# Latent attention: VectorE instead of ScalarE copies the last transposed probabilities of each head

## The reference, cut to what matters

```
for each block of 128 queries i (kv_len = (i+1)*128):
    s = q_nope @ k_nope^T + q_rope @ k_rope^T, times (64+32)^-0.5
    p = softmax(where(causal mask, s, -inf))
    o = p @ v                                   # 16 heads, v of width 64
o = o * silu(gate);  return o @ w_out
```

## Time and profile before

| | us |
|---|---|
| median of 3 runs | 1749.3 |
| lowest and highest | 1748.59, 1751.31 |
| the profiled execution, its own time | 1748.29 |
| its span, first to last instruction | 1746.5 |
| TensorE busy in the span | 1695.5 |
| VectorE busy | 1016.4 |
| ScalarE busy | 842.5 |
| GpSimd busy | 701.0 |

### The profile page before, as it was taken

One profiled execution on the slowest core, in us unless ns is written; L12 is line 12 of the kernel. 1 busy time (PEld: TensorE's weight loads), 2 busy tenths in 40 slices (PEclk: granted clock), 3 DMA queues, 4 the chain that ended last, 5 costly groups with the idle time before them and its releaser, 6 DMA issues.

```text
span 1746.5 us, 24655 instructions
## 1 busy us (share of the span) xinstructions
PE 1695.5 (97%) x8729; PEld 1380.8 (79%) x8729; DVE 1016.4 (58%) x1600; ACT 842.5 (48%) x1472; POOL 701.0 (40%) x795
## 2 busy tenths in 40 slices
PE   8999999989999999999989999999999999999998
PEld 6877777757786667878878888888888888888887
DVE  5578685687458855376658657877634443222222
ACT  5465665786366654356532345565423331313131
POOL 2634445426442014411123432324345455555554
PEclk9999999999999999999999999999999999999999
DMA  7362624223231002201048521112133223333333
GB/s 223 109 193 77 189 85 121 86 84 85 77 90 45 17 20 81 61 25 37 25 154 256 180 61 37 49 49 61 49 97 97 84 85 97 97 96 96 96 97 109
DMA packets 217151, 160.55 MB, mean 92 GB/s; under 512 B 8334, under 2 KB 190615, under 8 KB 217047
## 3 DMA queue, kind: packets, MB, share of 16 engines
q1 hardware_dynamic: 201758, 125.50, 25.0%
q10 hardware_dynamic: 15288, 33.66, 5.8%
HBM read 156.98 MB, written 2.16 MB: 91 GB/s over the span
## 4 chain that ended last, share of the span: by engine, by line
PE 65%; issue 12%; DVE 8%; ACT 7%; POOL 7%; DMA 1%; ACTq 0%; POOLq 0%; DVEq 0%; SPq 0%
PE ps L665 14%; PE ps L669 14%; PE ps L666 14%; POOL wl L615 7%; PE ps L3184 3%; PE ps L3182 3%; PE ps L3181 3%; PE ps L2238 2%; PE ps L2220 1%; PE ps L1685 1%; ACT wh L628 1%; PE ps L1653 1%; PE ps L2777 1%; PE ps L2227 1%; PE ps L2743 1%
## 5 line engine op out<-in xcount | busy, mean ns | idle before, releaser
L615 POOL TENSOR_TENSOR wl<-raw,wh 128x256 fp32r<-128x256 f32 (+1 forms) x775 | 677.6, 905 | 985.8 <-ACT wh L628 985.8
L665 PE MATMUL ps<-ah,wh 128*128 128x512 f32 (+1 forms) x1144 | 457.2, 400 | 8.3 <-DVE al L793 2.2
L669 PE MATMUL ps<-ah,wl 128*128 128x512 f32 (+1 forms) x1144 | 446.7, 390 | 0.2
L666 PE MATMUL ps<-al,wh 128*128 128x512 f32 (+1 forms) x1144 | 445.7, 390 | 0.0
L628 ACT ACTIVATE wh<-raw 128x1024 fp32r<-128x1024 f32 (+1 forms) x220 | 230.6, 1049 | 299.2 <-PE ps L669 153.3
L665 PEld LDWEIGHTS ps<-ah,wh 128*128 128x128 f32 (+1 forms) x1144 | 213.6, 187 | 62.5 <-issue 8.6
L669 PEld LDWEIGHTS ps<-ah,wl 128*128 128x128 f32 (+1 forms) x1144 | 213.4, 187 | 49.2 <-POOL wl L615 1.9
L666 PEld LDWEIGHTS ps<-al,wh 128*128 128x128 f32 (+1 forms) x1144 | 213.7, 187 | 43.8 <-issue 1.7
L665 PE MATMUL ps<-bh,wh 128*128 128x512 f32 (+1 forms) x332 | 134.1, 404 | 8.1 <-DVE merged L2639 2.8
L669 PE MATMUL ps<-bh,wl 128*128 128x512 f32 (+1 forms) x332 | 130.8, 394 | 0.8 <-POOL wl L615 0.7
L666 PE MATMUL ps<-bl,wh 128*128 128x512 f32 (+1 forms) x332 | 130.0, 392 | 0.0
(11 more groups left out here) (470 smaller groups left out, 2965.4 us busy)
## 6 DMA issues: line engine op xcount, KB each, us to landing
raw<-w_mlp SPq DMA_DIRECT2D x64, 512.0 KB, 3.9
raw<-w_in SPq DMA_DIRECT2D x52, 512.0 KB, 3.8
raw<-ssm_w_in SPq DMA_DIRECT2D x40, 512.0 KB, 3.9
ada_late<-w_ada ACTq DMA_DIRECT2D x16, 1024.0 KB, 7.0
ada_raw<-w_ada ACTq DMA_DIRECT2D x16, 512.0 KB, 4.7
cum_rows<-cum_saved ACTq DMA_DIRECT2D x16, 512.0 KB, 3.9
raw<-ssm_w_out SPq DMA_DIRECT2D x16, 512.0 KB, 3.4
raw<-mla_w_in SPq DMA_DIRECT2D x11, 512.0 KB, 4.0
```

What stands on the lines that cost most here:

```text
L615: nc.gpsimd.tensor_tensor(wl[:, s, part], raw[:, s, part], wh[:, s, part].bitcast(F32), ALU.subtract).then_inc(lo_ready, LOW_PIECES * (par ...
L665: nc.tensor.matmul(dst, w_hi[k], x_hi[k], start=k == 0, stop=False)
L666: nc.tensor.matmul(dst, w_hi[k], x_lo[k], start=False, stop=False)
L669: ins = nc.tensor.matmul(dst, w_lo[k], x_hi[k], start=False, stop=k == n - 1)
```

## The change

The copy of part 2 of each head goes from ScalarE's queue to VectorE's. VectorE makes it for head h-2 in `softmax(h)`, behind the second division, as one `tensor_copy` of 128x512 out of bank 6; in the last step it makes the two that are left. It waits for the transpose and, from head 2 on, for the outputs that read the same buffer. Part 0 and 1 stay on ScalarE.

```diff
                     exp(h + 1, 0)
                     exp(h + 1, 1)
-                if h:
-                    copy_turned(h - 1, 2)
                 if h + 1 < MH:
                     exp(h + 1, 2)
                     exp(h + 1, 3)
...
                 copy_turned(h, 1)
-            copy_turned(MH - 1, 2)
             gate_high(MH // 2 - 1)
...
+            def copy_last(h):
+
+                dve.wait_ge(sem("probs_turned"), h * 3 + 3)
+                if h > 1:
+                    dve.wait_ge(sem("o_ready"), h // 2)
+                nc.vector.tensor_copy(probs_t[h % 2][:, 0:TT, 3 * P:T], bank(6).rearrange("p (k n) -> p k n", n=P)).then_inc(sem("probs_copied"), 1)
+
             def softmax(h):
                 for t in range(TT):
                     top(h, t)
                     if t >= 2:
                         scale(h, t - 2)
+                if h > 1:
+                    copy_last(h - 2)
                 scale(h, TT - 2)
                 scale(h, TT - 1)
...
             for h in range(MH):
                 if h + 1 < MH:
                     softmax(h + 1)
+                else:
+                    copy_last(h - 1)
+                    copy_last(h)
                 if h % 2 == 0 and h:
                     gate(h // 2 - 1)
```

## The result

The changed kernel takes 1756.50 us (median of 6 runs, 1755.65 to 1759.36) against 1748.96 us for the kernel before in the same series: a ratio of 1.0043, 95% interval 1.0031 to 1.0055. It is slower by 7.5 us. Forecast were 1756.7 us, from a median before of 1749.3, and 7.4 us slower. The profiled execution took 1755.93 us with a span of 1754.1, 7.6 us over the span of before.

The account below looks back on a forecast made before the run. TensorE, busy 97% of the span, was taken as the bound. Delays of 2.08 + 5.04 + 0.19 + 0.09 gave 7.4 us slower, 1756.7 us against a median of 1749.3; range 1751 to 1763.

Parts of the forecast that it names:

- The copy starts 0.27 us behind the second division and takes 0.69: VectorE's queue: free 0.27 us after the second division's start; copy priced at 0.69 us from another 128x512 PSUM copy.
- Work starts 1.02 us behind the second division: TensorE's outputs or first transposes start 1.02 us after VectorE's second division starts, 0.06 us behind the copy's end.
- the replay: Attention loop retimed step by step from the timelines before, with the copy on VectorE: 7.4 us slower; chance 0.72.
- The queue is pushed by 0.41 us: VectorE's queue behind the copy: second to fourth division takes 1.60 us instead of 1.19, so 0.41 later, not 0.62.
- Steps 5 to 8: +0.71, +1.65, +2.19, +2.52: TensorE's running delay over four attention steps; 2.52 us per four steps, repeated by the next four.
- In step 7 ScalarE's queue shifts by 1.23 us: Fourth exponential, after head 8's fourth maximum, starts 1.23 us later; queries, weight split, gate and head 7's first copy follow.
- First four heads 2.08, last heads 0.19 and 0.09: Delays outside the eight replayed steps: +2.08 us first four, +0.19 at last heads' transposes, +0.09 for the final copy.
- Twelve stalls of 0.5 to 1.1 us, 9 to 12 in all: Profile sign: TensorE waits for VectorE's probs_t before outputs and first transposes, replacing 4.3 us of waits for ScalarE.
- ScalarE 9.6 us less busy, VectorE 11 more: Profile sign: moving the copies makes ScalarE 9.6 us less busy and VectorE 11 us more.
- the one in which VectorE's lateness accumulates: Second division of every step: no old wait absorbs VectorE's lateness; 11.4 us slower, 1760.7 us; chance 0.13.
- The rival of no measurable difference: Later waits inside the stage take the stalls back, or the copy starts at once; 0 to +3 us, 1751; chance 0.09.
- The one on the other side: Copy ready before TensorE's projection ends, so only ScalarE's relief remains; 4.7 us faster, 1744.6 us; chance 0.06.

Follow-up runs that it names:

- The run with the load alone: Kernel before plus an unrelated VectorE multiplication, as long as the copy, at its place in fourteen of sixteen heads; copies stay on ScalarE: 1751.30 us, ratio 1.0010.
- the run of the even heads: Changed kernel with only even heads' copies on VectorE, behind the second division; odd heads' copies back on ScalarE: 1749.32 us, ratio 0.9998 to the kernel before.
- that of the odd heads: Changed kernel with only odd heads' copies on VectorE, behind the second division; even heads' copies back on ScalarE: 1757.21 us, ratio 1.0040 to the kernel before.
- the run ahead of the first division: Changed kernel with VectorE's copy ahead of the first division instead of behind the second: 1752.82 us, ratio 1.0018 to the kernel before.
- the run with ScalarE's copy late: Kernel before with ScalarE's copy moved behind the fourth exponential, nothing given to VectorE: 1759.21 us, ratio 1.0055.

## Why the prediction was right

- **Nothing is given back outside the loop.** Forecast 7.4 us; the loop gave 7.5, the span 7.6, the medians 7.5. That the sum is off by only 0.1 us is partly luck: the terms below are too small by 0.2 us before step 12 and too large by 0.1 behind it, and the medians can't show 0.1 us at all.
- **The copy starts 0.27 us behind the second division and takes 0.69.** Measured 0.27 and 0.684 on average. VectorE's copy of another tile and line priced this one within 1%.
- **Work starts 1.02 us behind the second division.** Right for the outputs (582.02 to 583.03 is 1.01). For the transposes it is 1.10 (575.55 to 576.65): they followed 0.15 us behind the copy, not 0.06. This costs nothing, as the scores then followed 0.68 us behind the transposes (576.65 to 577.33) and not 0.79: they came 0.68 us late, where the replay has 0.71.
- **The queue is pushed by 0.41 us.** The second division of step 6 comes 0.40 us late (582.02 for 579.40, less the 2.22 by which the outputs at 568.12 are later). The run with the load alone agrees: 0.40 us per four steps.
- **Steps 5 to 8: +0.71, +1.65, +2.19, +2.52.** Counted from the outputs before them (568.12 now, 565.90 then), the outputs of step 6 come 1.63 late, the transposes of step 7 2.25 and the outputs of step 8 2.60. That an old wait pays part of step 5's stall (1.14 us at the transposes, 0.68 left at the scores), and that the outputs pay in full, was the core of the replay; the run of the even heads shows the first (0.12) and that of the odd heads the second (2.51).
- **In step 7 ScalarE's queue shifts by 1.23 us.** This is the mis-sized term. The fourth exponential comes 1.21 us late (589.87 for 586.44), but the copy of queries behind it 1.30 (590.62 for 587.10), and everything behind that 1.31 to 1.32, down to the second division of step 8 (597.19 for 593.65; all less the 2.22). The rows of TensorE, ScalarE and VectorE in the changed kernel:

```profile
590.19 0.40 PE L669 MATMUL ps<-bh,wl 128*128 128x512 f32 x1
589.87 0.69 ACT L1808 ACTIVATE probs<-ps,nmax 128x512 f32<-128x512 f32 x1
590.46 0.19 ACT L1808 ACTIVATION_READ_ACCUMULATOR probs<-ps,nmax 128x1 f32 x1
590.62 0.59 ACT L1795 ACTIVATE queries<-ps 64x512 f32<-64x512 f32 x1
...
597.19 0.35 DVE L1970 TENSOR_SCALAR probs<-probs,rinv 128x256 f32<-128x256 f32 x1
```

  That copy waits for TensorE's projection (L1786), which is 1.63 us late and ends at 590.59, 0.03 us before the copy starts; before, it ended at 586.73, 0.37 us ahead of it. The gap is too short for the profile to name what ended it, so this is read from the times. It makes four steps 2.60 us instead of 2.52.
- **First four heads 2.08, last heads 0.19 and 0.09.** Measured, less 0.07 by which the loop began later: 2.15 at 568.12; 0.09 between the outputs of steps 12 and 14 (13.52 for 13.43); 0.10 at the last outputs (8.08 for 7.98). The 0.19 was for the transposes of step 13: they came 0.27 us later (7.67 for 7.40 us behind the outputs of step 12), and 0.09 of it was left at the outputs of step 14.
- **Twelve stalls of 0.5 to 1.1 us, 9 to 12 in all.** Thirteen and 12.5 in the profile, a little over. Most lie between 0.46 and 1.20 us; two, of 1.43 and 1.76 us, are larger. They stand in the first four steps, for which I gave the sum and not the single stalls.
- **ScalarE 9.6 us less busy, VectorE 11 more.** Wrong in size: 6.3 less and 9.7 more in the whole kernel, 6.6 less and 7.8 more in the loop. I summed the durations of single instructions, but the page counts the union, and each of these copies overlaps the instruction ahead of it and the one behind it by some 0.1 us. On VectorE the copy starts at 575.82, before the division's end at 575.90, and the next instruction at 576.42, before the copy's end at 576.50.

Of the rivals, the one in which VectorE's lateness accumulates (11.4 us; its terms add up to 11.3) falls by the measured 7.5. VectorE still waits for the outputs before it gates them, longer than before; these are its rows in step 6 of the changed kernel and then of the kernel before:

```profile
585.45 0.69 DVE L1995 TENSOR_TENSOR norm_v<-ps,gates 128x512 f32<-128x512 f32 x1 [1.36 <-PE ps L1685]
```

```profile
581.60 0.69 DVE L1989 TENSOR_TENSOR norm_v<-ps,gates 128x512 f32<-128x512 f32 x1 [0.53 <-PE ps L1685]
```

And the even heads' stalls, 0.46 to 1.43 us each, end in 0.5 us for the whole loop. The rival of no measurable difference (0 to 3 us) falls too. The one on the other side (the copy ready in time, 4.7 us faster) needed the copy a microsecond sooner, and the run ahead of the first division shows why it isn't to be had: where the copy is in time, the maximum behind it is not. The Trainium skill (TensorEngine Tiling (Array Packing), PSUM Bottleneck) advises to use both ScalarE and VectorE for emptying PSUM, for a TensorE that tiling has made faster. Both already do it in the kernel before; giving VectorE sixteen more copies cost 7.5 us, and giving it three chosen ones shortened the loop by 1.0.

Judged by how busy VectorE is, nothing would be lost. It does idle 5.5 us in four steps of the changed kernel, and yet the steps take 2.6 us more.

## What to carry to other kernels

A moved instruction is priced by when its result is ready in its new queue against when the bound engine asks for it, not by its own duration or by how busy the new engine is: here 0.68 us of work a head, on an engine with 4.7 us to spare in four heads, cost 0.5 us a head. Work this out from two timelines, step by step, and look at each stall for an old wait just behind it, which pays for it. If some of such moves are nearly free and others are not, split them: moving only the three copies that were in ScalarE's way, to a place in VectorE's queue where they were in time, shortened the loop by about 1 us.

## What the runs showed of the hardware

In the run with the copy made twice, TensorE's clock fell at two places of the loop, each time for the output matmuls right behind a wait. Its timeline (outputs alone), and its table for the stretches before and at each place:

```profile
571.18 4.06 PE L1686 MATMUL ps<-probs_t,vals 128*64 128x512 f32 x16 [1.99 <-DVE probs_t L1979]
...
588.98 2.37 PE L1686 MATMUL ps<-probs_t,vals 128*64 128x512 f32 x16 [1.75 <-DVE probs_t L1979]
...
659.61 3.81 PE L1686 MATMUL ps<-probs_t,vals 128*64 128x512 f32 x16 [1.38 <-DVE probs_t L1979]
```

```profile
568.00:571.18 3.18, 1.19 (x6) 0.63 (x5) 3.05 (x9) 2.63 (x9) 0.21 (x1) 1.00 0.50 138
571.18:574.70 3.52, 3.52 (x14) 1.46 (x16) 0.99 (x4) 0.00 (x0) 0.00 (x0) 0.57 0.10 29
...
656.00:659.61 3.61, 1.72 (x13) 1.06 (x11) 1.55 (x4) 0.93 (x3) 0.00 (x0) 1.00 0.00 0
659.61:663.00 3.39, 3.39 (x16) 1.52 (x16) 0.54 (x1) 0.00 (x0) 0.00 (x0) 0.61 0.01 2
```

The same sixteen matmuls took 4.06 and 3.81 us against 2.37. The mean granted clock of the two stretches is 0.57 and 0.61 of full speed, so for most of them TensorE was at 1.2 GHz, the lower of its two levels, and it came back within a few microseconds. In the stretches before, TensorE had worked 1.19 of 3.18 and 1.72 of 3.61 us. A wait of 2.02 us in the same run (before the transposes at 548.28) and two of 1.75 us had no such effect, and in the loop of every other kernel, with waits up to 2.0 us (in the run with ScalarE's copy late), each 5 us have a clock of 1.00. What decides between them stays open. I had given the clock no term in the prediction, since the waits before were at most 0.9 us; the changed kernel, with waits of up to 1.8 us, needed none.
